# w_in products by one level of Strassen's scheme, with q/k/v/o and gates spilled to DRAM

## The reference

```python
h = rmsnorm(x, pre_w)
proj = h @ w_in                       # 1024 x 1024 @ 1024 x 12296
q_m, k_m, v_m, o_m, z_m, if_pre, q_a, k_a, v_a, z_a, g_m, g_a = split(proj)
# mLSTM branch: 4 heads of 256, chunks of 128 tokens
q_m, k_m = silu(conv4(q_m)), silu(conv4(k_m))
hm = mlstm_chunkwise(q_m, k_m / 16, v_m, i, log_sigmoid(f)) * sigmoid(o_m)
branch_m = (head_rmsnorm(hm) * silu(z_m)) @ w_pm
# attention branch: 3 groups (window 128/512/2048, dilation 1/4/16) x 4 heads of 128
o, m, l = windowed_attention(rope(q_a), rope(k_a), v_a)      # per group and head
att = sum_g(exp(m_g - max) * l_g * o_g) / sum_g(...)         # groups merged per head
branch_a = (att * silu(z_a)) @ w_pa
y = (sigmoid(g_m) * branch_m + sigmoid(g_a) * branch_a) @ w_out
out = x + rmsnorm(y, post_w)
```

## Time and profile before

| | before |
|---|---|
| median of 3 executions | 1526.83 us (1525.88 to 1527.52) |
| span of the profiled execution | 1524.9 us |
| PE busy | 1481.9 us, 97% |
| DVE busy | 729.6 us, 48% |
| ACT busy | 433.2 us, 28% |
| POOL busy | 380.7 us, 25% |
| chain that ended last | PE 91%, DVE 6%; L713 63%, L732 17% |
| DMA | 97.03 MB, mean 64 GB/s |

### The profile page before, as it was taken

One profiled execution on the slowest core, in us unless ns is written; L12 is line 12 of the kernel. 1 busy time (PEld: TensorE's weight loads), 2 busy tenths in 40 slices (PEclk: granted clock), 3 DMA queues, 4 the chain that ended last, 5 costly groups with the idle time before them and its releaser, 6 DMA issues.

```text
span 1524.9 us, 20051 instructions
## 1 busy us (share of the span) xinstructions
PE 1481.9 (97%) x8244; PEld 1294.2 (85%) x8244; DVE 729.6 (48%) x1167; ACT 433.2 (28%) x834; POOL 380.7 (25%) x230
## 2 busy tenths in 40 slices
PE   6999999998999899999999999999999999999997
PEld 5888888886888688998898899899888888888997
DVE  6766346447634757514763753563342221433213
ACT  6312222222232124223322433233232213221221
POOL 4211111111111111112343333334333321122120
PEclk9999999999999999999999999999999999999999
DMA  5211112231212122321221121122121122431412
GB/s 178 58 38 47 42 42 43 43 84 42 43 42 83 42 43 62 92 34 38 83 70 42 56 56 42 43 69 57 43 68 43 34 78 76 130 112 46 161 29 111
DMA packets 151907, 97.03 MB, mean 64 GB/s; under 512 B 25156, under 2 KB 144452, under 8 KB 151304
## 3 DMA queue, kind: packets, MB, share of 16 engines
q1 hardware_dynamic: 151816, 95.74, 23.3%
HBM read 85.08 MB, written 10.65 MB: 63 GB/s over the span
## 4 chain that ended last, share of the span: by engine, by line
PE 91%; DVE 6%; issue 1%; ACT 1%; DMA 0%; SPq 0%; DVEq 0%; POOL 0%; POOLq 0%; ACTq 0%
PE proj L713 63%; PE proj L732 17%; PE bank L757 2%; PE keep L782 2%; PE bank L831 2%; PE keep L831 1%; DVE share_sb L1351 1%; PE bank L820 1%; PE bank L768 1%; PE bank L795 1%; DVE tmp L1157 1%; DVE mqk L1186 0%; PE proj L744 0%; DMA x_sb<-x_in 0%; PE keep L825 0%
## 5 line engine op out<-in xcount | busy, mean ns | idle before, releaser
L645 POOL TENSOR_TENSOR wlo<-raw,whi 128x1024 fp32r<-128x1024 f32 (+1 forms) x120 | 282.6, 2356 | 1029.0 <-ACT whi L943 1029.0
L713 PE MATMUL proj<-hhi,whi 128*128 128x512 f32 x1280 | 401.1, 395 | 0.0
L713 PE MATMUL proj<-hlo,whi 128*128 128x512 f32 x1280 | 395.7, 390 | 0.0
L713 PE MATMUL proj<-hhi,wlo 128*128 128x512 f32 x1280 | 395.4, 390 | 0.0
L713 PEld LDWEIGHTS proj<-hlo,whi 128*128 128x128 f32 x1280 | 241.1, 188 | 50.8
L713 PEld LDWEIGHTS proj<-hhi,wlo 128*128 128x128 f32 x1280 | 240.8, 188 | 51.0
L713 PEld LDWEIGHTS proj<-hhi,whi 128*128 128x128 f32 x1280 | 237.2, 189 | 46.0
L732 PE MATMUL proj<-whi,hhi 128*128 128x256 f32 x512 | 146.5, 286 | 0.0
L732 PE MATMUL proj<-wlo,hhi 128*128 128x256 f32 x512 | 145.6, 284 | 0.0
L732 PE MATMUL proj<-whi,hlo 128*128 128x256 f32 x512 | 145.6, 284 | 0.0
L943 ACT ACTIVATE whi<-raw 128x1024 fp32r<-128x1024 f32 (+1 forms) x121 | 123.7, 1024 | 13.8 <-DMA raw<-w_pm 6.0
(11 more groups left out here) (219 smaller groups left out, 2014.4 us busy)
## 6 DMA issues: line engine op xcount, KB each, us to landing
raw<-w_in SPq DMA_DIRECT2D x96, 512.0 KB, 4.5
share_sb<-share_spill SPq DMA_DIRECT2D x4, 1536.0 KB, 9.6
x_sb<-x_in SPq DMA_DIRECT2D x8, 512.0 KB, 6.3
hm_spill<-mz SPq DMA_DIRECT2D x4, 1024.0 KB, 6.9
raw<-hm_spill SPq DMA_DIRECT2D x8, 512.0 KB, 3.3
raw<-w_pm SPq DMA_DIRECT2D x8, 512.0 KB, 4.0
raw<-w_out SPq DMA_DIRECT2D x8, 512.0 KB, 3.9
x_sb<-x_in SPq DMA_DIRECT2D x1, 4096.0 KB, 14.9
```

The source lines that it names most:

```text
L645: nc.gpsimd.tensor_tensor(low, src, hi.bitcast(F32), ALU.subtract).then_inc(lo_done, 1)
L713: mm = pe.matmul(slot[:, half * 512:(half + 1) * 512], w[:, ws, kt, :], m[:, kt, half * 512:(half + 1) * 512], start=(kt == 0 and w is whi ...
```

## The change

The w_in work is done in pairs of column tiles. With the input cut by k-tiles and by halves of the tokens into B11, B21 and B22 (and B12, which enters only through sums), and the two weight tiles into A11, A12 (first tile, lower and upper k-tiles), A21, A22 (second tile), seven products of 4 k-tiles x 3 parts = 12 matmuls over 512 tokens give both tiles. The weight sums S1 to S4 are made by GpSimd for every pair (`add`), the input sums T1 to T4 once at the start. Products of 48 pairs, 336 in all, form one sequence of steps; each engine's stream goes through the steps, and every other piece of work is attached to a step by a table. The four PSUM halves of `proj` are the accumulators: `a` (two, by pair), `b` and `c`.

Moved or added with it:
- Attention goes group by group in 10 slots of 2 or 4 query tiles per head; each group's values are turned just before. Masks are applied with the sign turned. ScalarE, not VectorE, copies turned probabilities and values.
- mLSTM q, k, v, o of a pair of tiles (after conv and silu) are staged in SBUF (3 slots) and written to DRAM (`m_spill`, 1 MB a pair); each chunk reads its 8 tiles of 128 tokens back (`chunk_in`). Values and output gates are now made in transposed form and turned by TensorE in each chunk. VectorE instead of GpSimd makes the values' low part.
- The conv taps read the staged tile in SBUF and add into `tmp`.
- The 16 gate tiles go to DRAM (`gate_spill`) and are read back one by one in the tail.
- Shares of the groups are loaded group by group, 512 KB each.
- Weights for the tail are split in buffers of their own.

The core of the diff: the sequence and tables, GpSimd's low parts, TensorE's product, what ScalarE and then VectorE do after a product, and the sums at the start.

```diff
-SLOT_QUANTA = (1, 1, 1, 2, 1, 1, 1, 2)
-WSLOTS = 4
+RING = 4
+LEAD = RING - 1
+BANKS = 3
+PRODUCTS = {
+    "P1": ("A11", "B11", "a"),
+    "P2": ("A12", "B21", "c"),
+    "P6": ("S2", "T2", "a"),
+    "P5": ("S1", "T1", "b"),
+    "P7": ("S3", "T3", "a"),
+    "P4": ("A22", "T4", "a"),
+    "P3": ("S4", "B22", "b"),
+}
+HEAD_PAIRS = ((("k", 0), ("v", 0)), (("q", 0), ("v", 1)), (("k", 1), ("q", 1)),
+              (("k", 2), ("v", 2)), (("z", 0), ("q", 2)))
+SLOT_AT = (18, 20, 23, 25, 28, 30, 33, 35, 39, 41)
+SLOT_UNIT = (0, 0, 0, 0, 1, 1, 1, 1, 2, 2)
+NSLOT = len(SLOT_AT)
+TURN_AT = {0: 8, 1: 15, 2: 30}
+def plan_products(npairs):
+    seq = [(0, "P1")]
+    for p in range(npairs):
+        seq += [(p, n) for n in ("P2", "P6", "P5", "P7")]
+        if p + 1 < npairs:
+            seq.append((p + 1, "P1"))
+        seq += [(p, "P4"), (p, "P3")]
+    return seq
...
+        base = 35 * h
+        for i, s in enumerate(SLOT_AT):
+            items[base + s + 3].append(("pv", h, i))
+        for i, s in enumerate(SLOT_AT):
+            items[base + s + 2].append(("probT", h, i))
+        for g, s in TURN_AT.items():
+            for half in range(2):
+                items[base + s + half].append(("vT", h, g, half))
+        for i, s in enumerate(SLOT_AT):
+            items[base + s].append(("scores", h, i))
+        for kind, g, at in (("k", 0, 8), ("q", 0, 15), ("q", 1, 22), ("k", 1, 24), ("k", 2, 29), ("q", 2, 35)):
+            for piece in range(2):
+                dve_late[base + at + piece].append(("rope", h, kind, g, piece))
...
+        sp_late[base + 43].append(("ml_out", h))
+        sp_late[base + 44].append(("ml_in", h))
+        dve_late[base + 46].append(("compare", h))
+        act_late[base + 46].append(("eg", h))
+        dve_late[base + 47].append(("shares", h))
+        sp_late[base + 48].append(("share_out", h))
+        sp_late[base + 49].append(("share_in", h, 0))
+        sp_late[base + 49].append(("share_in", h, 1))
+        dve_late[base + 52].append(("combine", h, 0))
+        dve_late[base + 53].append(("combine", h, 1))
+        sp_late[base + 54].append(("share_in", h, 2))
+        dve_late[base + 57].append(("combine", h, 2))
+        dve_late[base + 58].append(("combine", h, 3))
...
+    for h, (first, gap) in enumerate(((175, 3.5), (203, 4.375), (238, 4.375), (273, 3.5))):
+        for n in range(NT):
+            start_of[h, n] = int(first + gap * n)
+    chunks = sorted(start_of, key=lambda c: start_of[c])
+    for h, n in chunks:
+        s = start_of[h, n]
...
+        free = start_of[chunks[c - 2]] + 2 if c > 1 else 171
+        sp_late[max(free, ready)].append(("chunk_in", h, n))
+        items[s].append(("start", h, n))
+        items[s + 2].append(("end", h, n))
+        pool_late[s].append(("queries", h, n))
+        act_late[s + 3].append(("square", h, n))
+        if n < NT - 1:
+            act_late[s + 3].append(("state", h, n + 1))
+            pool_late[s + 3].append(("state", h, n + 1))
+    tmp_no = {}
...
+        if kind in ("mq", "mk"):
+            for j, a in ((1, 7), (0, 10)):
+                tmp_no[p, j] = len(tmp_no)
+                act_late[at + a].append(("conv", p, j))
+                dve_late[at + a + 1].append(("taps", p, j, (1,)))
+                dve_late[at + a + 2].append(("taps", p, j, (2, 3)))
+                act_late[at + a + 2].append(("conv_tanh", p, j))
+                dve_late[at + a + 3].append(("silu", p, j))
+            sp_late[at + 14].append(("spill", p))
...
+            def low(k):
+                p, name = seq[k]
+                src = operand(p, PRODUCTS[name][0])
+                g.wait_ge(hi_done, k + 1)
+                TT(w_lo_ring[k % RING][:], src, w_hi_ring[k % RING][:].bitcast(F32), ALU.subtract
+                   ).then_inc(lo_done, 1)
...
+            for k in range(NSTEP):
+                if k + LEAD < NK:
+                    low(k + LEAD)
+                p = k // 7
+                if k % 7 == 4 and p + 1 < NP:
+                    add(p + 1, "S1")
+                    add(p + 1, "S2")
+                if k % 7 == 5 and p + 1 < NP:
+                    add(p + 1, "S3")
+                if k % 7 == 1 and p < NP:
+                    add(p, "S4")
...
+            def product(k):
+                p, name = seq[k]
+                w_name, b, which = PRODUCTS[name]
+                pe.wait_ge(lo_done, k + 1)
+                if name == "P1" and p >= 2:
+                    pe.wait_ge(c21_done, p - 1)
+                elif name == "P6":
+                    pe.wait_ge(s1_done, p + 1)
+                elif name == "P5" and p:
+                    pe.wait_ge(c12_done, p)
+                elif name == "P2" and p:
+                    pe.wait_ge(c11_done, p)
+                elif name == "P7":
+                    pe.wait_ge(u2_done, p + 1)
+                elif name == "P4":
+                    pe.wait_ge(u3_done, p + 1)
+                elif name == "P3":
+                    pe.wait_ge(c22_done, p + 1)
+                wh, wl = w_hi_ring[k % RING], w_lo_ring[k % RING]
+                first = name in ("P1", "P2", "P5")
+                for kt in range(4):
+                    if p == 0:
+                        pe.wait_ge(h_ready[b], kt + 1)
+                    for w, m in ((wh, h_hi[b]), (wh, h_lo[b]), (wl, h_hi[b])):
+                        mm = pe.matmul(acc(p, which), w[:, kt, :], m[:, kt, :],
+                                       start=(first and kt == 0 and w is wh and m is h_hi[b]),
+                                       stop=(kt == 3 and w is wl), skip_group_check=True)
+                mm.then_inc(pe_prod, 1)
...
+            def after(k):
+                p, name = seq[k]
+                if name not in ("P1", "P6", "P7", "P4"):
                     return
+                act.wait_ge(pe_prod, k + 1)
+                a = acc(p, "a")
+                if name == "P1":
+                    if p:
+                        act.wait_ge(c22_done, p)
+                    A(snap[0][:], a, ACT.Copy).then_inc(s1_done, 1)
+                elif name == "P6":
+                    if p:
+                        act.wait_ge(c12_done, p)
+                    A(snap[1][:], a, ACT.Copy).then_inc(u2_done, 1)
+                elif name == "P7":
...
+            def after(k):
+                p, name = seq[k]
+                if name == "P2":
+                    tile, d = place(p, 0)
+                    dve.wait_ge(pe_prod, k + 1)
+                    dve.wait_ge(s1_done, p + 1)
+                    place_wait(dve, p, 0)
+                    TT(half_view(tile, d, 0), token_view(snap[0][:], d), token_view(acc(p, "c"), d), ALU.add
+                       ).then_inc(c11_done, 1)
+                elif name == "P7":
+                    tile, d = place(p, 1)
+                    dve.wait_ge(u3_done, p + 1)
+                    place_wait(dve, p, 1)
+                    TT(half_view(tile, d, 1), token_view(snap[0][:], d), token_view(acc(p, "b"), d), ALU.add
+                       ).then_inc(c22_done, 1)
+                elif name == "P3":
+                    tile, d = place(p, 0)
+                    dve.wait_ge(pe_prod, k + 1)
+                    dve.wait_ge(u2_done, p + 1)
+                    TT(half_view(tile, d, 1), token_view(snap[1][:], d), token_view(acc(p, "b"), d), ALU.add
+                       ).then_inc(c12_done, 1)
...
+            def second_half(j):
+                w = prew[:, j:j + 1]
+                dve.wait_ge(pe_ht, KT + 2 * j + 1)
+                dve.wait_ge(b_done, KT)
+                STT(h_sum["T1"][:, j, :], ht2_bank[j], w, b_sb[:, j, :], ALU.mult, ALU.subtract
+                    ).then_inc(h_sum_done, 1)
+                dve.wait_ge(b_done, KT + j + 1)
+                STT(h_sum["T3"][:, j, :], ht2_bank[j], w, h_sum["B22"][:, j, :], ALU.mult, ALU.subtract
+                    ).then_inc(h_sum_done, 1)
+                dve.wait_ge(h_sum_done, 4 * j + 2)
+                TT(h_sum["T2"][:, j, :], h_sum["B22"][:, j, :], h_sum["T1"][:, j, :], ALU.subtract
+                   ).then_inc(h_sum_done, 1)
+                dve.wait_ge(h_sum_done, 4 * j + 3)
+                TT(h_sum["T4"][:, j, :], b_sb[:, 4 + j, :], h_sum["T2"][:, j, :], ALU.subtract
```

2568 lines of the change are left out of this document (1469 added, 1099 removed).

## The result

The changed kernel takes **1564.66 us** (median, 1563.74 to 1567.05) where the kernel before takes 1526.59 us on the same chip: ratio **1.0252**, 95% interval 1.0238 to 1.0267. It is slower by 38 us.

What follows compares the result with a forecast made beforehand. TensorE, busy 1481.9 of 1524.9 us, was taken as the bound. 1524.9 - 140.5 (matmuls) + 14 (transposes) + 15 (start) + 10 (end) - 24 (old stalls) gave 1399, or 1401 on the median's scale; plus 78 of stalls: 1480 us, range 1425 to 1555.

Steps and rivals of the forecast that it cites:

- Matmuls removed, 140.5 us: w_in projections on TensorE: 1057.8 us of matmuls become 336 products taking 917.3 us, which takes off 140.5 us.
- (c): Rival: w_in matmuls' column count does not fall; with one-bank matmuls slower by 50 us, 1530 us; chance 0.03.
- 12 us on the clock, for eight gaps: TensorE's granted clock drops behind gaps of 2 us, some 1.5 us lost each; eight such stalls, 12 us.
- The attention heads, stalls of 6 us each, 2 more for the maxima and some clock: VectorE bursts at steps 22 to 25 stall three heads 6 us each; maxima's DRAM exchange costs 2 us in four heads.
- Head 0, 10 us for the gate rows: First attention head, steps 9 to 19: 31 us of VectorE gate rows beside two ropes stall TensorE 10 us.
- The start, 15 us: Before products run densely: VectorE's input sums and GpSimd's low parts come late, losing 15 us, bounds 8 and 22.
- The end, 10 us: Tail: the last gate tiles' trip through DRAM and queued loads ahead of a w_pa weight cost 10 us, bounds 3 and 16.
- GpSimd, 650 to 720 us: Sign that the forecast is right: GpSimd's busy time over the whole kernel near 650 to 720 us.
- the third of the loads, mLSTM with the conv: mLSTM heads: VectorE 107 of 122 us a head, 53 us over in six conv pairs; 22 us reach TensorE.
- 8 for the banks in heads 0 and 3: mLSTM heads with chunks three or four steps apart: output-gate transposes wait for a bank VectorE frees, 8 us.
- Rival (a): Whole kernel: GpSimd's three products of lead and two banks' slack cover bursts; stalls 0 to 49 us; chance 0.27.
- Rival (b): Late ScalarE snapshots leave gaps that lower TensorE's clock, 4 us a time; 40 such give 1561 us, slower; chance 0.19.

Runs made afterwards that it cites:

- e11_neither: Changed kernel with GpSimd's four sums of w_in blocks and the lower halves of w_in's products both left out (output not the reference's): 1447.6 us, ratio 0.9484.

## Why the prediction was wrong, step by step

- **Matmuls removed, 140.5 us: right.** 4032 matmuls of 512 columns stand in the trace, 12 of them in 2.74 us, so one bank costs nothing and (c) is out. But TensorE's busy time fell by 83 us and not by the 126.5 that follow from my terms (140.5 less 14): the same matmuls ran at a mean granted clock of 0.959. I had put 12 us on the clock, for eight gaps.
- **The attention heads, stalls of 6 us each, 2 more for the maxima and some clock: right in size.** A head without a stall is 116.6 us by my terms and 126.1 was measured. Its parts were off: the load was worth 5.5 us (126.1 to 120.6), the maxima's exchange under 1.
- **Head 0, 10 us for the gate rows: somewhat small.** From product 7 to 35 TensorE idles for 14.4 of 115.1 us (busy 100.7), at a clock of 0.96; the load holds 10.9 us of that stage.
- **The start, 15 us: about 30.** TensorE's long wait there, 12.12 us, ends at 59.14 us with ScalarE's snapshot of P1 (58.47 to 59.04 us), which stood behind the roundings of the token sums, and these behind VectorE's sums. I had put a sum at 0.75 us; with two operands in SBUF the last ones took 1.54 and 1.64 us. The terms also forgot that the lower halves of T4 and B22, 8 operations of VectorE at 1.7 us beside GpSimd, come before the first addition that frees a bank (72.83 us), but TensorE waited only 1.58 us behind that. Moving the snapshot and the weights gave nothing; leaving out GpSimd's load gave 5.3 us, and 9.91 us of the long wait stayed. What the rest is made of stays open.
- **The end, 10 us: about 6.** In the window behind the last product TensorE is busy for 44.8 of 50.8 us.
- **GpSimd, 650 to 720 us: wrong, 942.** I multiplied 528 operations by the median of 1.31 us. Their medians are still about 1.30, but the means run from 1.44 to 1.71 (single ones up to 3.28 us, where VectorE holds GpSimd up in turn as in the earlier trace rows), so that they took 800 us and not 692. And I left out what GpSimd did besides, 155 us; 13 us of all this overlap.
- **The step that failed is the third of the loads, mLSTM with the conv: 22 us and 8 for the banks in heads 0 and 3.** I had counted 24 us of port waits in a head and let them fall into slack. The stages from product 140 to 301 lose 75.8 us by GpSimd's load alone (639.8 against 564.0 us). VectorE's instructions are 210 us longer beside that load than without it, over the whole kernel; my rows 8 and 9 had shown the mechanism, one operation of 0.27 us taking 1.79, and I priced it as an average of 0.5 us on 64 operations, when operations with two operands in SBUF met it whatever their size, down to one of a single column (its median is 1146 ns, its least 159):

```profile
881.77 1.28 POOL L902 TENSOR_TENSOR w_lo<-raw,w_hi 128x512 fp32r<-128x512 f32 x1 [1.32 <-ACT w_hi L1285]
...
881.93 1.14 DVE L1913 TENSOR_TENSOR den<-den,cols 128x1 f32<-128x1 f32 x1
```

The one-column maximum began 0.16 us behind GpSimd's subtraction and ended with it.
- **Rival (a), the feeders keep up, 1401 to 1450 us**, is what only e11_neither shows (1447.6), at the upper edge: with GpSimd's load gone, all other new waits together cost 47 us over the base of 1401.
- **Rival (b), 1561 us, has the number, by luck, and half of the mechanism.** The clock did fall to 0.93 and 0.94 in the first three mLSTM heads (0.98 in the last), and the tanh did wait for taps. But ScalarE's snapshot released TensorE in only 12 us of its idle time, and moving the tanh gave 3.6 us. The gaps had their source one engine further back.

Summed up: 164 us lie between the base of 1401 and 1564.7, where I had 78. GpSimd's load holds 117 of them; of my 78, the terms that were such load (bursts in three attention heads: 18, gate rows: 10, conv: 22, banks in heads 0 and 3: 8) came to 58.

## What to carry to other kernels

Before work goes to an engine because that engine idles, ask what it shares: here a microsecond of two-operand work on GpSimd cost 0.125 to 0.20 us of the changed kernel and 0.136 us of the one before, though in the changed kernel GpSimd was busy for only 60% of the time and VectorE for 59%. Price it in the trace by the mean and not the median of the operations that already overlap, and by leaving the work out once: one run here gave the answer that four reorderings could not. Orders are worth trying again once the load is right: a new order of one chain of roundings gave 3 us under the full load and another order of the same chain gave 11 us after. Whether the second would have given as much before was not tried.
